# Moving four modulation chunks of layer two from layer one's experts to layer two's attention

## The chip, the cores and the metric

The kernel runs on one core of one Trainium2 chip. The metric is the device time of one execution in microseconds (us), taken as the median of a few runs. "PE" is the tensor engine (matrix products), "PEld" its loading of weights, "DVE" the vector engine, "ACT" the scalar engine, "SP" the engine whose queue issues nearly all loads from memory. The tensor engine's clock has two levels, 1.2 and 2.4 GHz; the profile gives the granted clock as a share of the higher one.

## The reference

Two blocks of two layers each are computed, one behind the other, on 256 tokens of width 1024 in 32-bit floats. The change is in the first block. For each of its layers:

```python
c_act = silu(c)                                  # one row of 1024
mod = c_act @ w_ada[l] + b_ada[l]                # 6 * 1024 numbers
sh_m, sc_m, g_m, sh_f, sc_f, g_f = split(mod, 6)
h = x * (1 + sc_m) + sh_m
mix = token_mixers(h, ...)                       # attention, retention, mLSTM, output product
x = layer_norm(ALPHA * x + (1 + g_m) * mix, ln_mix_g[l], ln_mix_b[l])
h = x * (1 + sc_f) + sh_f                        # <- shift and scale of the feed forward part
y = moe_ffn(h, ...)                              # router and 16 experts, all computed
x = layer_norm(ALPHA * x + (1 + g_f) * y, ln_ffn_g[l], ln_ffn_b[l])
```

The modulation depends only on `c`, so each of its pieces can be computed at any time before its use. `w_ada[l]` is 1024 x 6144; the kernel cuts it into twelve chunks of 512 columns. Chunks 0 and 1 give `sh_m`, 2 and 3 `sc_m`, 4 and 5 `g_m`, 6 and 7 `sh_f`, 8 and 9 `sc_f`, 10 and 11 `g_f`.

## The kernel before

**One chunk.** A chunk is a load of 2 MB from `w_ada` into one slot of a ring (`load_ada`), then eight DVE instructions that multiply the eight row blocks by `cact` and add them up in `tmp` (`ada`: one `tensor_scalar` and seven `scalar_tensor_tensor`, L1376), then a sum over the 128 partitions on PE: four products of a 128 x 128 piece with a column of ones, each in two passes, so eight entries in the profile (`mix_sum`, L705, in the attention; `expert_sum`, L747, in the experts), then one short DVE instruction that adds the bias column (`sum_columns`). When the last of the four chunks is in, `fold("ffn", ...)` multiplies scale and shift with the gain and bias of the layer norm ahead (three short DVE instructions). Two buffers in `tmp` take turns, so a chunk's accumulation waits for the sum of the chunk two before it.

**Where chunks are done.** Three tuples say it. `EARLY` lists chunks done before anything else (layer one's 0 to 3), `MIXING` the chunks done in a layer's attention, `DURING` the chunks done in the expert loop: expert number, then `("ada", c)` for a chunk of this layer or `("next", c)` for one of the next layer. Before, layer one does 4 to 9 in its attention, and in its experts its own 10 and 11 and layer two's 0 to 3 and 6 to 9; layer two does 4 and 5 in its attention and 10 and 11 in its experts.

**The ring.** All weights but those of the down products pass through the four slots of `gring`, in one fixed order (`ring_order`). Entry n goes into slot n % 4, and its load waits until entry n - 4 has been used (`free_slot`, `last_use`): a projection's weights are free when its product for the second token half is done on PE, a chunk when its accumulation is done on DVE. The SP queue issues loads strictly in this order, so a load that waits holds up all behind it.

**The attention stage.** PE runs a written-out sequence (`pe_first`): projections `idx`, `aq`, `ak`, `av`, `mqk`; then eight attention steps s = 0 to 7. In each, PE computes scores (L860), transposes the probabilities (L868), does the work of `between(s)`, and multiplies by the values (L883). `between` holds halves of the projections `mvo` (s = 0 to 3) and `rqk` (s = 4 to 7, L534), at s = 5 the gate columns (L918), and at s = 7 the first mLSTM scores (`ml_scores(0)`, L928), which need the convolution's result after its SiLU on ACT. Then come `rvg` (L534), the mLSTM and retention heads and the output product (L1006). In layer one `mix_sum(6, 7)` stands at s = 2, `mix_sum(7, 6)` at s = 5, `mix_sum(8, 4)` and `mix_sum(9, 1)` behind; the second number is the PSUM bank. Bank 6 also holds the gate columns before and the second half of `rqk` after `mix_sum(7, 6)`.

DVE runs its own written-out order (`dve_first`): after `att_in(2)` come the two gate sums and `ada_of(6)`; after `att_in(3)` `gate_sums`; after `att_in(4)` `ada_of(7)` and `columns_of(6)`; then `att_in(5)`, `att_in(6)`, `att_out(0)`, `conv(0)`, `conv(1)`, `att_in(7)`, `gate_columns`, `conv(2)`, `columns_of(7)`, the rotation of `rqk`, `conv(3)`; at s = 7 `ada_of(8)`; after the mLSTM weights `columns_of(8)` and `ada_of(9)`. `ada_of(c)` and `columns_of(c)` do nothing when chunk c is not in the layer's tuple. Two things differ in layer two: `gain_and_bias` runs there twice (two passes over 128 x 1024 numbers each, L1373), once behind `gate_sums` and once between `att_in(4)` and `ada_of(7)`, and the small `wr_parts` instruction of layer one, behind `conv(3)`, does not run.

**The expert stage.** For each of 16 experts PE does 48 products for gate and up, 24 for down, and transposes (L651). Where `DURING` has a chunk, `expert_sum` follows the transposes of the next expert.

Of the kernel before, what the change touches and what calls it, by code (L numbers as in the profile page):

```python
# [17 lines left out]
KT = D // P  # L18
# [55 lines left out]

EARLY = ((0, 1, 2, 3), ())
EARLY_K = 1
MIXING = ((4, 5, 6, 7, 8, 9), (4, 5))

IN_DOWN = ("avcv", "ak", "buv", "cqk", "wo0")
DIFF = [(t, h) for t in range(TT) for h in range(DH)]  # L80
# [4 lines left out]
MIX_ORDER = (2, 3, 0, 1)  # L85

DURING = (
    {1: ("ada", 10), 2: ("ada", 11), 4: ("next", 0), 5: ("next", 1), 6: ("next", 2), 7: ("next", 3), 9: ("next", 6),
     10: ("next", 7), 12: ("next", 8), 13: ("next", 9)},
    {1: ("ada", 10), 2: ("ada", 11)},  # L90
)

# [7 lines left out]
def ring_order():  # L100

    order = []
    for l, s in enumerate(FIRST):
        names = {0: "ada0 ada1 ada2 ada3 idx aq ada4 ak ada5 av ada6 mqk ada7 mvo ada8 rqk ada9 rvg wo0 wo1",
                 1: "idx aq ak ada4 av ada5 mqk mvo rqk rvg wo0 wo1"}[l].split()
        for e in range(NE):
            names.append(f"gu{e}")
            if e - 1 in DURING[l]:
                names.append(during(l, e - 1))
        order += [(s, n) for n in names]  # L110
    for s in SECOND:
        order += [(s, n) for n in ["avcv", "aq", "ak", "buv", "cqk", "wo0", "wo1"]]
        order += [(s, f"gu{e}") for e in range(NF)] + [(s, "pg0"), (s, "pg1")]
    return order
# [17 lines left out]
B_ADA, LN_MIX_G, LN_MIX_B, LN_FFN_G, LN_FFN_B = 0, 96, 112, 128, 144  # L132
# [104 lines left out]
def program(nc, ins, out, known):  # L237
    ctx = ExitStack()
    with ctx:
# [166 lines left out]
        av, rvg = buf(TT, N), buf(TT, N)  # L406
# [53 lines left out]
        mod = [sc(KT) for _ in range(4)]  # L460
# [230 lines left out]
        def pe_first(l):  # L691
# [255 lines left out]
            def between(s):  # L947

                if s < 4:
                    half_in_proj("mvo", s // 2, s % 2)  # L950
                if s == 2:
                    if l == 0:
                        mix_sum(6, 7)
                if s == 4:
                    half_in_proj("rqk", 0, 0)
                if s == 5:
                    gate_columns()
                    half_in_proj("rqk", 0, 1)
                    if l == 0:
                        mix_sum(7, 6)  # L960
                if s == 6:
                    half_in_proj("rqk", 1, 0)
                if s == 7:
                    ml_scores(0)
                    half_in_proj("rqk", 1, 1)
# [11 lines left out]
                att_values(s)  # L977
            for h in range(NR):
                half_in_proj("rvg", h // 2, h % 2)
                if h == 2 and l == 0:  # L980
                    mix_sum(8, 4)
                if h == 0:
                    ml_scores(1)
                if h < 2:
                    transposed_rope("rqk", h, 4, 4)
                if h == NR - 1:
                    pe.wait_ge(vector_done, V.at(T, ("read", ("att", "O", 1))))
                    transposed_mix(range(2), A)
                ml_values(h)
                if h + 2 < NR:  # L990
                    ml_scores(h + 2)
# [19 lines left out]
            ret_scores(0)  # L1011
            ret_scores(1)
            output_part(0, 0, "att")
            if l == 0:
                mix_sum(9, 1)
            ret_values(0)
            ret_values(1)
            ret_scores(2)
# [630 lines left out]
        def dve_first(l):  # L1649
# [262 lines left out]
            tt(hflat, hflat, mo, ALU.mult).then_inc(vector_done, V.step())  # L1912
            dve.wait_ge(vector_done, V.now())
            columns_of(9)
            if l == 0:
                fold("ffn", LN_MIX_G, LN_MIX_B, mod[3], mod[2])
            ret_weights(2)
            ret_weights(3)
            head_variance("ml", hn, sq, hs, hv)
# [82 lines left out]
            def read_sum(e):  # L2002
# [3 lines left out]
                kind, c = DURING[l][e - 1]  # L2006
# [3 lines left out]
                else:  # L2010
                    sum_columns(l + (kind == "next"), c, psum[:, 2, 0:4], name)
                    if c == 3:
                        fold("mix", LN_FFN_G + KT * l, LN_FFN_B + KT * l, mod[1], mod[0])
                    if c == 9:
                        fold("ffn", LN_MIX_G + KT * (l + 1), LN_MIX_B + KT * (l + 1), mod[3], mod[2])

            def chunk(e):

# [1143 lines left out]
```

## Time and profile before

| what | us |
| --- | --- |
| runs: lowest, median, highest | 1688.45, 1688.72, 1691.14 |
| profiled execution, first to last instruction (span) | 1680.9 |
| median minus that span | 7.8 |
| PE busy in the span | 1626.5 |
| DVE busy | 1083.0 |
| ACT busy | 715.9 |

The profiled execution has no timed figure of its own beside its span; the 7.8 us is what lies outside the first and last instruction when it is compared with the median of the runs. Times in rows are us from the span's start. A timeline row has start, length, engine, line, operation, output <- input, shapes and count; what stands in square brackets is the engine's idle time just ahead and what ended it.

### The profile page before, as it was taken

To read this page: it belongs to the slowest core of one execution; us is meant where nothing else is said; L and a number is where in the kernel's file an instruction comes from. 1 tells how busy PE (TensorE), PEld (TensorE's weight loads), DVE (VectorE), ACT (ScalarE), POOL (GpSimd) and SP (SyncE) were. 2 spreads that over 40 slices of the span, in tenths; PEclk is the share of its full clock that TensorE was granted. 3 is DMA by queue.
4 is the path that set the end of the run, shared out by engine and by line. 5 is a ranking of instruction groups with operands and counts; after the bars stand their busy time and mean duration, and the time that the engine had idled before them with its cause. 6 is when DMAs were issued, how large, how long until landed. Compare 5 with 4: busy or idle time off the path is not lost.

```text
span 1680.9 us, 19186 instructions
## 1 busy us (share of the span) xinstructions
PE 1626.5 (97%) x7467; PEld 1237.3 (74%) x7467; DVE 1083.0 (64%) x1692; ACT 715.9 (43%) x1105; POOL 0.2 (0%) x4
## 2 busy tenths in 40 slices
PE   6999999999999999999999989899999998999998
PEld 5465577888885655688888878778887887788886
DVE  8676787867656764884545567864546767754446
ACT  1133343434321233433434346754336756643445
POOL 0000000000000000000000000000000000000000
PEclk9999999999999999999999999999999998999999
DMA  9846357878664722556555662146466451444641
GB/s 352 303 180 246 126 189 261 289 262 286 228 231 163 249 107 95 188 200 216 184 175 200 208 176 101 51 152 219 155 212 213 146 190 51 150 151 161 215 165 49
DMA packets 218682, 314.98 MB, mean 187 GB/s; under 512 B 22484, under 2 KB 147804, under 8 KB 218464
## 3 DMA queue, kind: packets, MB, share of 16 engines
q1 hardware_dynamic: 217904, 313.63, 54.3%
q8 instruction: 59, 0.97, 0.2%
q14 instruction: 31, 0.25, 0.0%
q10 hardware_dynamic: 688, 0.13, 0.0%
HBM read 312.70 MB, written 1.05 MB: 187 GB/s over the span
## 4 chain that ended last, share of the span: by engine, by line
PE 84%; DVE 10%; ACT 3%; DMA 1%; issue 1%; SPq 0%; DVEq 0%; ACTq 0%
PE psum L598 18%; PE psum L599 17%; PE psum L600 17%; PE psum L534 9%; PE psum L1006 3%; PE psum L605 2%; DVE gring_parts L1373 1%; PE psum L651 1%; DVE arena L1373 1%; PE psum L1206 1%; PE psum L574 1%; DVE arena L1376 1%; PE psum L517 1%; PE psum L575 1%; PE psum L554 1%
## 5 line engine op out<-in xcount | busy, mean ns | idle before, releaser
L600 PE MATMUL psum<-arena_parts,hT_parts 128*128 128x512 f32 x896 | 352.6, 393 | 0.0
L1373 DVE TENSOR_TENSOR gring_parts<-gring,arena_parts 128x2048 fp32r<-128x2048 f32 (+1 forms) x125 | 278.9, 2271 | 50.7 <-ACT arena_parts L2412 50.3
L2412 ACT ACTIVATE arena_parts<-gring 128x2048 fp32r<-128x2048 f32 (+1 forms) x125 | 231.3, 1904 | 7.0 <-DMA gring<-in_w_up 6.6
L1373 DVE TENSOR_TENSOR arena_parts<-psum,ex_parts 128x256 fp32r<-128x256 f32 x106 | 44.6, 420 | 281.0 <-ACT ex_parts L2412 280.9
L2412 ACT ACTIVATE ex_parts<-psum 128x256 fp32r<-128x256 f32 x106 | 40.5, 382 | 394.2 <-PE psum L651 394.2
L598 PE MATMUL psum<-arena_parts,o_cat_parts 128*128 128x512 f32 x512 | 203.2, 397 | 0.0
L599 PE MATMUL psum<-gring_parts,o_cat_parts 128*128 128x512 f32 x512 | 201.8, 394 | 0.0
L600 PEld LDWEIGHTS psum<-arena_parts,hT_parts 128*128 128x128 f32 x896 | 168.2, 188 | 39.4
L598 PE MATMUL psum<-arena_parts,ex_parts 128*128 128x512 f32 x424 | 177.3, 418 | 0.3 <-DVE arena_parts L1373 0.3
L534 PE MATMUL psum<-gring,hT 128*128 128x512 f32 x384 | 174.7, 605 | 1.8 <-DMA gring<-in_w_in 1.8
L600 PE MATMUL psum<-arena_parts 128*128 128x512 f32 x432 | 169.9, 393 | 0.0
L599 PE MATMUL psum<-dring_parts,ex_parts 128*128 128x512 f32 x424 | 166.6, 393 | 0.0
L599 PE MATMUL psum<-gring_parts,arena_parts 128*128 128x512 f32 x416 | 163.9, 394 | 0.0
L598 PE MATMUL psum<-arena_parts 128*128 128x512 f32 x392 | 155.1, 396 | 0.6 <-DVE gring_parts L1373 0.6
L534 PEld LDWEIGHTS psum<-gring,hT 128*128 128x128 f32 x384 | 71.8, 193 | 82.4 <-issue 79.3
L1376 DVE SCALAR_TENSOR_TENSOR tmp<-gring,cact,tmp 128x512 f32<-128x512 f32 x164 | 123.3, 752 | 7.3 <-DMA gring<-in_w_ada 1.2
L1373 DVE TENSOR_TENSOR dring_parts<-dring,arena_parts 128x2048 fp32r<-128x2048 f32 x54 | 123.5, 2287 | 4.4 <-ACT arena_parts L2412 4.4
L2412 ACT ACTIVATE arena<-psum 128x512 f32<-128x512 f32 (+2 forms) x92 | 50.6, 553 | 158.5 <-PE psum L534 74.5
L598 PEld LDWEIGHTS psum<-arena_parts,o_cat_parts 128*128 128x128 f32 x512 | 96.1, 188 | 22.9 <-DVE hT_parts L1373 0.5
L599 PEld LDWEIGHTS psum<-gring_parts,o_cat_parts 128*128 128x128 f32 x512 | 96.2, 188 | 22.5 <-issue 0.5
L2412 ACT ACTIVATE arena_parts<-dring 128x2048 fp32r<-128x2048 f32 x54 | 103.2, 1912 | 0.0
L600 PEld LDWEIGHTS psum<-arena_parts 128*128 128x128 f32 x432 | 81.1, 188 | 19.2
(268 smaller groups left out, 2371.3 us busy)
## 6 DMA issues: line engine op xcount, KB each, us to landing
gring<-in_w_ffn_in SPq DMA_DIRECT2D x44, 1024.0 KB, 8.8
gring<-in_w_ada SPq DMA_DIRECT2D x20, 2048.0 KB, 9.9
gring<-in_w_in SPq DMA_DIRECT2D x16, 2048.0 KB, 12.7
gring<-in_w_gate SPq DMA_DIRECT2D x32, 1024.0 KB, 7.4
gring<-in_w_up SPq DMA_DIRECT2D x32, 1024.0 KB, 9.8
dring<-in_w_down SPq DMA_DIRECT2D x32, 1024.0 KB, 5.1
dring<-in_w_ffn_out SPq DMA_DIRECT2D x22, 1024.0 KB, 5.0
gring<-in_w_out SPq DMA_DIRECT2D x8, 2048.0 KB, 8.3
```

What stands on the lines that cost most here:

```text
L517: last = nc.tensor.matmul(ps[:, 0:n], hT[:, k, t * P:(t + 1) * P], w[:, k, 0:n], start=k == 0, stop=k == KT - 1)
L534: last = nc.tensor.matmul(ps[:, 0:n], hT[:, k, t * P:(t + 1) * P], w[:, k, 0:n], start=k == 0, stop=k == KT - 1)
L554: nc.tensor.matmul(o, w[:, k % 4, c0:c0 + P], hi[:, :, k, :], start=first and k == 0, stop=False)
L574: nc.tensor.matmul(ps, hi[:, t, k, :], w, start=started and k == 0, stop=False)
L598: nc.tensor.matmul(ps, hi, w, start=start, stop=False)
L599: nc.tensor.matmul(ps, hi, w_rest, start=False, stop=False)
L600: return nc.tensor.matmul(ps, lo, w, start=False, stop=stop)
L605: last = nc.tensor.matmul(ps[0:m, at:at + SEQ], w[:, k, c0:c0 + m], hT[:, k, :], start=k == 0, stop=k == KT - 1)
L1006: last = nc.tensor.matmul(ps, hT[:, k, t * P:(t + 1) * P], gslot(stage, f"wo{h}")[:, k, 0:N], start=k == 0, stop=k == 5)
L1373: return nc.vector.tensor_tensor(o, a, b, op)
L1376: return nc.vector.scalar_tensor_tensor(o, a, s, b, op0, op1)
L2412: return nc.scalar.activation(o, a, ACT.Copy)
```

## The change

Chunks 6 to 9 of layer two leave layer one's `DURING` and join layer two's `MIXING`; the ring order, the sums on PE, and the fold on DVE follow.

```diff
-MIXING = ((4, 5, 6, 7, 8, 9), (4, 5))
+MIXING = ((4, 5, 6, 7, 8, 9), (4, 5, 6, 7, 8, 9))
 DURING = (
-    {1: ("ada", 10), 2: ("ada", 11), 4: ("next", 0), 5: ("next", 1), 6: ("next", 2), 7: ("next", 3), 9: ("next", 6),
-     10: ("next", 7), 12: ("next", 8), 13: ("next", 9)},
+    {1: ("ada", 10), 2: ("ada", 11), 4: ("next", 0), 5: ("next", 1), 6: ("next", 2), 7: ("next", 3)},
     {1: ("ada", 10), 2: ("ada", 11)},
 )
...
-                 1: "idx aq ak ada4 av ada5 mqk mvo rqk rvg wo0 wo1"}[l].split()
+                 1: "idx aq ada4 ak ada5 av ada6 mqk ada7 mvo ada8 rqk ada9 rvg wo0 wo1"}[l].split()
...
                 if s == 2:
-                    if l == 0:
-                        mix_sum(6, 7)
+                    mix_sum(6, 7)
...
-                    if l == 0:
-                        mix_sum(7, 6)
+                    mix_sum(7, 6)
...
-                if h == 2 and l == 0:
+                if h == 2:
                     mix_sum(8, 4)
...
-            if l == 0:
-                mix_sum(9, 1)
+            mix_sum(9, 1)
...
             columns_of(9)
-            if l == 0:
-                fold("ffn", LN_MIX_G, LN_MIX_B, mod[3], mod[2])
+            fold("ffn", LN_MIX_G + KT * l, LN_MIX_B + KT * l, mod[3], mod[2])
...
-                    if c == 9:
-                        fold("ffn", LN_MIX_G + KT * (l + 1), LN_MIX_B + KT * (l + 1), mod[3], mod[2])
```

With it, layer two has the ring order up to its experts that layer one has from `idx` on.

## Rows read from the trace of the kernel before

**Rows 1.** The page, busy us (share) and instructions of each engine.

```profile
PE 1626.5 (97%) x7467; PEld 1237.3 (74%) x7467; DVE 1083.0 (64%) x1692; ACT 715.9 (43%) x1105; POOL 0.2 (0%) x4
```

**Rows 2.** The page, chain that ended last, shares by engine.

```profile
PE 84%; DVE 10%; ACT 3%; DMA 1%; issue 1%; SPq 0%; DVEq 0%; ACTq 0%
```

**Rows 3.** Windows: stretch, length, busy of PE, PEld, DVE, ACT, POOL, clock, DMA.

```profile
104.39:186.47 82.08, 79.38 (x337) 46.51 (x335) 57.39 (x108) 26.57 (x56) 0.00 (x0) 0.98 0.53 190
581.18:657.68 76.50, 75.64 (x305) 42.87 (x303) 37.83 (x72) 29.26 (x57) 0.00 (x0) 0.98 0.37 127
232.00:500.00 268.00, 267.27 (x1215) 216.46 (x1214) 191.74 (x224) 98.22 (x105) 0.00 (x0) 1.00 0.72 252
```

**Rows 4.** Timeline of PE in layer one's experts, with and without a chunk.

```profile
326.42 0.38 PE L651 MATMUL psum<-cshared,ex 128*128 128x128 f32 x2
326.63 0.95 PE L747 MATMUL psum<-ones,tmp 128*128 128x1 f32 x8
344.48 0.38 PE L651 MATMUL psum<-cshared,ex 128*128 128x128 f32 x2
...
398.66 0.38 PE L651 MATMUL psum<-cshared,ex 128*128 128x128 f32 x2
415.82 0.38 PE L651 MATMUL psum<-cshared,ex 128*128 128x128 f32 x2
```

**Rows 5.** Timeline of PE in layer one's attention.

```profile
129.05 5.31 PE L534 MATMUL psum<-gring,hT 128*128 128x512 f32 x8 [1.78 <-DMA gring<-in_w_in]
...
140.86 0.95 PE L705 MATMUL psum<-ones,tmp 128*128 128x1 f32 x8
...
147.31 0.61 PE L868 MATMUL psum<-cshared,arena 128*128 128x128 f32 x4
148.69 0.69 PE L928 MATMUL psum<-ex,crows 4*128 4x256 f32 x2 [0.77 <-ACT arena L2409]
...
196.07 3.70 PE L1006 MATMUL psum<-gring,hT 128*128 128x512 f32 x8 [0.69 <-ACT hT L2412]
```

**Rows 6.** Timeline of PE in layer two's attention.

```profile
603.01 3.60 PE L534 MATMUL psum<-gring,hT 128*128 128x512 f32 x8
...
619.99 0.69 PE L928 MATMUL psum<-ex,crows 4*128 4x256 f32 x2 [0.71 <-ACT arena L2409]
...
633.97 5.40 PE L534 MATMUL psum<-gring,hT 128*128 128x512 f32 x8
...
667.28 3.70 PE L1006 MATMUL psum<-gring,hT 128*128 128x512 f32 x8 [0.69 <-ACT hT L2412]
```

**Rows 7.** Timeline of SP's queue, layer one: the loads of chunk 8 and `rqk`.

```profile
115.93 0.37 SPq L2933 DMA_DIRECT2D gring<-in_w_ada  x1
116.40 0.52 SPq L2933 DMA_DIRECT2D gring<-in_w_in  x1
```

**Rows 8.** Timeline of SP's queue, layer two: the loads of `rqk` and `rvg`.

```profile
565.74 0.99 SPq L2933 DMA_DIRECT2D gring<-in_w_in  x2
```

**Rows 9.** Timeline of DVE in layer one: chunk 6, `att_in(7)`, `columns_of(7)`, end of `conv(3)`.

```profile
110.36 5.47 DVE L1376 SCALAR_TENSOR_TENSOR tmp<-gring,cact,tmp 128x512 f32<-128x512 f32 x7
...
136.56 0.69 DVE L1376 SCALAR_TENSOR_TENSOR arena<-psum,arena 128x512 f32<-128x512 f32 x1 [1.49 <-PE psum L868]
...
141.92 0.16 DVE L1373 TENSOR_TENSOR small<-psum,pcol 128x4 f32<-128x4 f32 x1 [1.73 <-PE psum L705]
...
144.68 1.53 DVE L1376 SCALAR_TENSOR_TENSOR arena<-arena,pcol 128x256 f32<-128x256 f32 x3
```

**Rows 10.** Timeline of DVE in layer two: one of two `gain_and_bias`.

```profile
592.28 2.48 DVE L1373 TENSOR_TENSOR x<-x,rows 128x1024 f32<-128x1024 f32 x2
```

**Rows 11.** Windows (columns as in group 3): the granted clock behind layer one's wait.

```profile
129.00:132.00 3.00, 2.95 (x4) 1.40 (x5) 2.83 (x6) 2.87 (x10) 0.00 (x0) 0.50 1.01 378
```

**Rows 12.** Timeline of PE in the second block: a transposition behind a wait.

```profile
1067.42 0.96 PE L1182 MATMUL psum<-cshared,arena 128*128 128x128 f32 x4 [1.34 <-ACT arena L2412]
```

## The prediction

> **What bounds the kernel now.** I read the page first. PE is busy for 1626.5 of 1680.9 us [rows 1] and carries 84% of the chain that ended last, DVE 10% [rows 2]. So each us of PE work or PE waiting on that chain counts in full, and DVE work counts only where PE ends up waiting for it. Then I read the two stages that the change touches by windows. In layer one's experts PE is busy for 267.27 of 268.00 us, with DVE at 191.74 [rows 3]: there is almost no wait to win. In the attentions the two windows run from the transpositions and sums ahead of the eight steps to the third attention part of the output product, the same work in both layers but for what this change moves. Layer one takes 82.08 us with PE idle for 2.70, layer two 76.50 with PE idle for 0.86 [rows 3]. Layer one already carries chunks 6 to 9 in the very places and ring order that the change gives layer two, so its trace is the best measure of what is added. Last, I read the timelines of PE, DVE and SP side by side, shifted by 581.18 - 104.39 = 476.79 us.
>
> **Removed from the experts.** PE's transpositions mark the experts. With a chunk the distance is 344.48 - 326.42 = 18.06 us, without 415.82 - 398.66 = 17.16 us [rows 4]. The 0.90 us are the sum's own eight products (0.95 long, overlapping their neighbours). Four chunks leave: 4 x 0.90 = 3.60 us gained. DVE loses 4 x (0.5 + 5.5) = 24 us there (one multiply and seven additions, 5.47 for the seven [rows 9]), worth nothing by itself, since PE hardly waits in that stage. The four loads of 2 MB leave too; PE waits for no load there. At the end of the stage the first four loads of layer two now wait only for gate and up products of experts 12 to 15, the last (`ak`) for expert 15's, and PE takes idx, aq and the boundary's norm before it needs `ak`: nothing. Later ring entries fall into the same slots as before, since four entries left and four came in.
>
> **Added to layer two's attention, as layer one shows it.** 82.08 - 76.50 = 5.58 us [rows 3]. It can be split. (a) Four sums at 0.9 = 3.6. (b) PE waits 1.78 for the weights of `rqk` in layer one [rows 5], and not in layer two [rows 6]. The reason is SP's order: chunk 8's load waits for chunk 6's accumulation, and `rqk`, behind it, goes out at 116.40 [rows 7], lands 12.65 us later and is used at once. Layer two has no chunk 8 ahead of it, and issued it at 565.74 [rows 8], 37 us before its use. With the change it would go out at 116.40 + 476.79 - 3.60 and be as late as in layer one; all that precedes (ring, PE, DVE up to chunk 6) is layer one's order with layer one's durations. (c) After its wait layer one's eight products took 5.31 us where 3.60 is usual [rows 5, 6], and the granted clock was 0.50, the lower level of 1.2 GHz [rows 11]: 1.71. (d) Layer two has a slow stretch too, 5.40 for 3.70 at 633.97 with no wait ahead [rows 6]: -1.70. Sum 3.6 + 1.78 + 1.71 - 1.70 = 5.39; the last 0.2 is spread over starts and handovers. The later part costs nothing more: chunk 9 delays the load of the first expert's weights, and ACT's rounding of them, but from the end of the windows to the wait at 196.07 and 667.28 both layers take the same 9.6 us with the same idle of 0.69 [rows 5, 6]. If ACT came later there, PE would wait for the head norm's root, but layer one shows it just in time. The three instructions of `fold` are moved from one place to another on DVE, ahead of a wait for retention scores: nothing.
>
> **What layer one does not show.** DVE in layer two has two `gain_and_bias`, of 2.48 (2.52 with the gap) each [rows 10]: 5.04 us. Before, they stand in the place that chunks 6 and 7 have in layer one. With the change DVE has both. I follow DVE from chunk 6 to the end of `conv(3)`. Layer one: 110.36 to 146.21 = 35.85 us, of which it waits 1.49 and 1.73 [rows 9]; 32.63 of work. Layer two: 32.63 + 5.04 = 37.67, from 110.36 + 476.79 = 587.15, so the end is at 624.82, if DVE never waits; on the way each score that it needs is there 0.5 us or more ahead. PE's first mLSTM scores came 148.69 - 146.21 = 2.48 behind that end in layer one (a table load and SiLU on ACT [rows 5, 9]), so they start at 627.30, against 148.69 + 476.79 = 625.48 by layer one's pattern: 1.82 us later. Behind the waiting scores stand PE's second half of `rqk` and everything after it. So PE's wait there grows from 0.77 to 2.6 us in all; 0.9 of it comes earlier, at the sum of chunk 7: that sum takes bank 6, which DVE's copy of the gate columns frees only behind the late `att_in(7)`: 136.56 - 1.49 + 476.79 + 5.04 = 616.9 for its start, 1.6 for it and the copy, so 618.5, where PE is ready at 140.86 + 476.79 = 617.65. That part is not added a second time, as PE is caught by the same DVE end either way. From there DVE's chunk 8 ends at 630.9, and PE's `rqk` that it needs next at 632.4: DVE is no longer late. The bounds of this term: 0, if some DVE work fits into gaps that I took as gone; 5.04, if all of `gain_and_bias` came through. I take 1.82, the sum of the rows.
>
> **The clock.** Whether it falls is the uncertain part. It fell behind the wait of 1.78 [rows 5, 11], and behind one of 1.34 with thin work around it (a transposition group of 0.96 [rows 12]); it did not fall behind layer one's 0.77, and did fall at 633.97 with none. Layer two now gets waits of 0.9 and about 1.6 within 9 us, with small products between, ahead of the stretch where it fell before. I take one fall behind the `rqk` wait, as in (c), and one in the later stretch, where before there was one too. So the -1.70 of (d) does not apply, and the stage costs 5.58 + 1.82 + 1.70 = 9.10 us. The bounds: no fall at all leaves 9.10 - 3.4 = 5.7; three falls make it 10.8.
>
> The Trainium skill (TensorE: Matmul & The Clock Gate, section "What's actually happening") says that the point at which the clock changes is run-variable, since the gate does not start with the kernel. The trace agrees that equal work can differ: 633.97 fell and layer one's equal products did not.
>
> **Sum.** -3.60 + 9.10 = +5.5 us on the profiled execution's 1680.9, with the 7.8 us outside it unchanged: the median goes from 1688.72 to 1694.2. DVE's and ACT's totals stay what they were. The measurement tells about 0.2%, 3.4 us, from no change.
>
> **Rivals.**
> 1. No second fall of the clock: +5.5 - 1.7 = +3.8, 1692.5. For it: layer one fell only once. Against: the waits at 618 to 627 are longer than layer one's.
> 2. The pair of loads lands later than in layer one. The two issues at 115.93 and 116.40 moved 4 MB in 12.6 us; a load that takes 10% longer in that place adds 1.2: 1695.4. The same with a third fall of the clock is 1697.1.
> 3. The waits don't open up: `rqk` lands in time (it would have to be 1.8 us, 14%, faster than in layer one), so neither the wait nor its fall of the clock comes: 5.5 - 1.78 - 1.71 = +2.0, 1690.7, no change that can be measured. Against it is that every event before is layer one's.
> 4. Faster than before: the four sums hide in waits that PE has in layer two's attention anyway (0.71 and 0.69 [rows 6]), the loads are in time, and the clock no longer falls at 633.97. Then the attention pays 3.6 - 1.4 - 1.7 = 0.5 against 3.60 gained: -3.1, 1685.6. It decides from `rqk` landing before PE asks, and from DVE reaching `conv(3)` by 618. Against it: both waits end on DVE and ACT chains that the chunks lengthen.
>
> The Trainium skill (DMA: Bandwidth & Descriptors, section "Specifications") gives about 358 GB/s as what one core gets from memory. By it the 4.19 MB of the pair would take an estimated 11.7 us of moving alone, and with the start from issue to first byte the wait would be about a us longer than layer one's, as in rival 2. The trace does not support it as a limit: the window at that place averages 378 GB/s [rows 11].
>
> **How the numbers follow.** Forecast 0.46, rival 1 0.25, rival 2 0.08, rival 3 0.16, rival 4 0.05. To each I give 0.7 us of scatter, as the three runs of before lie from 0.3 below to 2.4 above their median. Range: from rival 3's 1690.7 less that scatter, 1690.0, to rival 2's upper value, 1697.0; it leaves out rival 4 and the ends. The forecast's own range is 1693.3 to 1695.1. Slower by over 3.4 us (above 1692.1): the forecast, rival 2 and four fifths of rival 1, 0.74; within: 0.22; faster 0.04.
>
> **What would show it.** In layer one's experts every distance from expert 9 on is 17.16. PE waits some 1.8 us for a load ahead of its first `rqk` product near 602 (all times 3.6 earlier than above), with the clock at 0.5 behind it. DVE has no wait from chunk 6 to `conv(3)`; chunk 7's sum waits about 0.9 and the first mLSTM scores about 1.6. The attention from 577.6 on is 9 us longer than before (7.4 in rival 1). The forecast is wrong if the wait for `rqk` is missing, if `conv(3)` ends before PE has done step 7, or if the expert stage shortens by more than 3.6: then DVE or the loads had cost PE time there that the rows do not show.

## The result and the profile after

| kernel | median us | runs | ratio to before, 95% interval |
| --- | --- | --- | --- |
| before | 1690.23 | 13 | 1 |
| changed | 1697.39 | 13 | 1.0048, 1.0034 to 1.0062 |

The change costs 8.1 us (5.7 to 10.5), where 5.5 were forecast. The time, 1697.39, lies 0.4 us above the range's upper end. The sign was right, the size was not. One execution of the changed kernel, the profiled one, and two of the one before ran disturbed (5684, 4309 and 2026 us): the medians in the table count them, the ratio does not, and it compares 1696.87 with 1688.72. The views below are of a second series of the changed program (1694.11 us, ratio 1.0042, 1.0028 to 1.0055).

The page of the changed kernel: busy time, the granted clock in 40 slices, and the chain that ended last. They answer to [rows 1, 2].

```profile
span 1693.2 us, 19182 instructions
PE 1635.0 (97%) x7467; PEld 1243.8 (73%) x7467; DVE 1083.2 (64%) x1692; ACT 715.8 (42%) x1105; POOL 0.2 (0%) x4
PEclk9999999999999999999999999899999998999999
PE 84%; DVE 10%; ACT 3%; DMA 2%; issue 1%; SPq 0%; DVEq 0%; ACTq 0%
```

PE has the same 7467 instructions and is busy 8.5 us longer. Equal products have become longer; how much of that is the clock is counted below. DVE and ACT are unchanged, as forecast.

The span grew by 1693.2 - 1680.9 = 12.3 us, more than the medians differ. The windows that answer to [rows 3], in the same order. The first and the third are layer one's and layer two's attention, each between the same two instructions as before; the second covers the same times as before:

```profile
104.03:187.98 83.95, 81.12 (x337) 47.19 (x336) 57.39 (x108) 26.56 (x56) 0.00 (x0) 0.96 0.52 186
232.00:500.00 268.00, 267.27 (x1199) 216.00 (x1198) 170.58 (x195) 99.84 (x107) 0.00 (x0) 1.00 0.65 224
580.04:665.67 85.63, 81.38 (x337) 47.06 (x335) 61.89 (x111) 26.27 (x55) 0.00 (x0) 0.96 0.50 182
```

Layer two's attention takes 85.63 - 76.50 = 9.13 us more; 9.10 were forecast. An expert that lost its chunk answers to [rows 4], in PE's timeline:

```profile
417.32 0.38 PE L650 MATMUL psum<-cshared,ex 128*128 128x128 f32 x2
...
434.48 0.38 PE L650 MATMUL psum<-cshared,ex 128*128 128x128 f32 x2
```

An expert has two such rows, so from the first shown to the last is one expert: 434.48 - 417.32 = 17.16 us. From expert 9 on every distance is so, and with a chunk it was 18.06. Four chunks give the forecast 3.60 back.

PE in layer two's attention, which answers to [rows 5, 6]: start of the stage, first half of `rqk`, product with the values of step 4, sum of chunk 7, first mLSTM scores, a projection at the lower clock, and the stage's end.

```profile
580.04 1.88 PE L701 MATMUL psum<-tmp,ones 128*128 128x512 f32 x4
...
605.84 5.40 PE L533 MATMUL psum<-gring,hT 128*128 128x512 f32 x8 [2.93 <-DMA gring<-in_w_in]
611.29 1.10 PE L882 MATMUL psum<-arena 128*128 128x64 f32 x8
...
618.06 0.95 PE L704 MATMUL psum<-ones,tmp 128*128 128x1 f32 x8
...
626.23 0.69 PE L927 MATMUL psum<-ex,crows 4*128 4x256 f32 x2 [1.12 <-ACT arena L2402]
...
640.31 5.26 PE L533 MATMUL psum<-gring,hT 128*128 128x512 f32 x8
...
665.67 3.70 PE L1003 MATMUL psum<-gring,hT 128*128 128x512 f32 x8
```

The `rqk` wait is there, 2.93 rather than 1.78, with the clock fallen behind it (5.40 for 3.60). The mLSTM wait is 1.12, not 1.6 or more, and the sum of chunk 7 doesn't wait. The loads of chunk 8 and `rqk` go out as late as forecast, `rqk` 12.02 us into the stage and 12.01 in layer one (the rows below and [rows 3, 7]). `rqk` is used 13.8 us after its issue, 12.65 in layer one [rows 5, 7]. On SP's queue, against [rows 8]:

```profile
591.58 0.37 SPq L2926 DMA_DIRECT2D gring<-in_w_ada  x1
592.06 0.52 SPq L2926 DMA_DIRECT2D gring<-in_w_in  x1
```

What the forecast did not have is outside this stage. These are windows over stretches where the granted clock (third number from the end) fell, first of the kernel before, then of the changed one. 0.50 is the level of 1.2 GHz, 1.00 that of 2.4; a window that also holds some full clock shows a value between.

```profile
128.00:134.00 6.00, 4.95 (x8) 2.26 (x9) 5.65 (x11) 3.29 (x10) 0.00 (x0) 0.72 1.02 360
634.00:638.00 4.00, 4.00 (x7) 1.70 (x7) 0.44 (x1) 0.00 (x0) 0.00 (x0) 0.57 0.00 0
...
1066.00:1072.00 6.00, 4.47 (x25) 4.27 (x24) 5.54 (x16) 4.07 (x11) 0.00 (x0) 0.72 0.00 0
```

```profile
148.00:152.00 4.00, 4.00 (x8) 1.79 (x7) 2.73 (x4) 1.21 (x3) 0.00 (x0) 0.57 0.00 2
162.00:166.00 4.00, 4.00 (x9) 1.94 (x8) 1.00 (x3) 0.00 (x0) 0.00 (x0) 0.57 0.99 386
506.00:512.00 6.00, 5.00 (x12) 3.33 (x13) 5.34 (x14) 1.08 (x4) 0.00 (x0) 0.72 0.24 90
606.00:610.00 4.00, 4.00 (x6) 1.68 (x7) 3.79 (x7) 0.60 (x2) 0.00 (x0) 0.58 0.27 49
640.00:644.00 4.00, 4.00 (x8) 1.80 (x7) 0.69 (x2) 0.00 (x0) 0.00 (x0) 0.57 1.06 406
...
1076.00:1092.00 16.00, 14.08 (x59) 13.05 (x60) 12.16 (x30) 9.77 (x22) 0.00 (x0) 0.57 0.00 1
```

Layer one's attention, whose code the change leaves alone, falls twice here and once before. The layer boundary falls (506), where before it did not, though PE's waits there are the same in both (1.18 and 1.29 us). In the second block a stretch of 6 us became one of 16, while one of 8 us before (972) is 6 us here (980). Stage by stage the pair of profiles adds up so: up to the end of layer one's attention +1.5 (187.98 against 186.47), experts -3.6, from the boundary to 580.04 +1.0, layer two's attention +9.1, and behind it +4.3 (1027.5 against 1023.2 us); in all +12.3. Windows of 2 us over the whole span count the lost clock, each window's length times one minus its clock: 16.5 us before and 24.8 in the changed kernel. The 8.3 between them are 1.7 each in layer one's attention, at the boundary and in layer two's attention, and 3.1 behind it. They agree with the 8.5 of PE's busy time.

One more number sorts these. For every execution, span x (1 - mean granted clock) is an estimate of the time lost to the lower level, and the rest is about what the program would take without it, waits included. It counts time at the lower level as lost even where PE waits, so it is rough by a us or so. Means over the executions:

| kernel | runs | span less lost | lost to the clock |
| --- | --- | --- | --- |
| before, three series | 23, 26, 23 | 1662.5, 1663.2, 1663.0 | 23.7, 23.8, 22.5 |
| changed, two series | 12, 6 | 1667.2, 1667.7 | 27.5, 24.8 |

Of the 8 us, about 4.5 are work and waits, about 3 more lost clock. The profile of before (16.5 lost) is thus of a lucky execution, 7 us below its program's mean of 23.4, and the changed kernel's (24.8) is 2 below its own of 26.6. So some 5 of the 8.3 us of clock between the two profiles are the choice of executions, and a fall in layer one's attention or in the second block cannot be put down to the change from this pair.

### The profile page after: what moved, and what is told of

Its sections match the earlier page's. It is cut to its first block, busy times and chain, and to the rows that moved or that the text cites. A ratio compares the mean times of both kernels' runs of the same rounds, so it can differ in the third digit from the quotient of the medians.

```text
span 5682.3 us, 19182 instructions
## 1 busy us (share of the span) xinstructions
PE 5662.5 (100%) x7467; PEld 2970.5 (52%) x7467; DVE 1095.4 (19%) x1692; ACT 725.5 (13%) x1105; POOL 0.2 (0%) x4
## 4 chain that ended last, share of the span: by engine, by line
PE 100%; DMA 0%; DVE 0%; ACTq 0%; ACT 0%; issue 0%; SPq 0%; DVEq 0%
PE psum L597 20%; PE psum L599 20%; PE psum L598 20%; PE psum L533 11%; PE psum L1003 4%; PE psum L604 2%; PE psum L1202 2%; PE psum L650 2%; PE psum L574 1%; PE psum L580 1%; PE psum L573 1%; PE psum L516 1%; PE psum L553 1%; PE psum L554 1%; PE psum L555 1%; PE psum L1178 1%
## 5 line engine op out<-in xcount | busy, mean ns | idle before, releaser
L599 PE MATMUL psum<-arena_parts,hT_parts 128*128 128x512 f32 x896 | 979.6, 1093 | 0.0
L533 PE MATMUL psum<-gring,hT 128*128 128x512 f32 x384 | 640.2, 1931 | 0.0
L599 PEld LDWEIGHTS psum<-arena_parts,hT_parts 128*128 128x128 f32 x896 | 383.2, 428 | 349.8 <-issue 349.6
L597 PE MATMUL psum<-arena_parts,o_cat_parts 128*128 128x512 f32 x512 | 564.9, 1103 | 0.0
L598 PE MATMUL psum<-gring_parts,o_cat_parts 128*128 128x512 f32 x512 | 559.7, 1093 | 0.0
L597 PE MATMUL psum<-arena_parts,ex_parts 128*128 128x512 f32 x424 | 494.5, 1166 | 0.0
L599 PE MATMUL psum<-arena_parts 128*128 128x512 f32 x432 | 473.3, 1095 | 0.0
L598 PE MATMUL psum<-dring_parts,ex_parts 128*128 128x512 f32 x424 | 463.8, 1094 | 0.0
L598 PE MATMUL psum<-gring_parts,arena_parts 128*128 128x512 f32 x416 | 454.9, 1093 | 0.0
L597 PE MATMUL psum<-arena_parts 128*128 128x512 f32 x392 | 431.0, 1099 | 0.0
L599 PEld LDWEIGHTS psum<-arena_parts 128*128 128x128 f32 x432 | 185.2, 429 | 168.2 <-issue 168.2
L597 PEld LDWEIGHTS psum<-arena_parts 128*128 128x128 f32 x392 | 168.3, 429 | 153.2 <-issue 151.8
```

The lines of the kernel that those rows point to most:

```text
L533: last = nc.tensor.matmul(ps[:, 0:n], hT[:, k, t * P:(t + 1) * P], w[:, k, 0:n], start=k == 0, stop=k == KT - 1)
L597: nc.tensor.matmul(ps, hi, w, start=start, stop=False)
L598: nc.tensor.matmul(ps, hi, w_rest, start=False, stop=False)
L599: return nc.tensor.matmul(ps, lo, w, start=False, stop=stop)
```

## The experiments

**The two programs again.** No edit. `changed_again`:

> The changed kernel as it is, for a profile that can be laid beside that of before. My theory (the waits): in layer two's attention PE waits about 1.8 us for the weights of rqk at s = 4 with the clock at its lower level behind it, 0.9 us at the sum of chunk 7, 1.6 us ahead of the first mLSTM scores; the stage is 9 us longer and the experts of layer one 3.6 shorter. Rival (the clock alone): the waits are as small as in the kernel before, and the extra time lies in stretches of 1.2 GHz, also outside the attention of layer two. Ratio to before expected 1.003 to 1.006 by both; what the windows show tells them apart.

`before_again`:

> The kernel before, unchanged. Its 13 runs lie in two groups, 1683 to 1684 and 1688 to 1693, and its profile has a span of 1680.9, which belongs to the lower group, as 1.8 us lie outside the span in the runs of the changed kernel. Theory: the groups differ in how often the clock falls, mean granted clock 0.990 in the lower and about 0.986 in the upper. If this profile is of the upper group it has some 6 us more in stretches of the lower level than the first profile. Rival: the groups differ in waits for loads, and the clock is the same. Ratio 1.000 within 0.002 by both.

Measured: changed 1694.11 (1.0042, 1.0028 to 1.0055), before 1688.34 (0.9993, 0.9980 to 1.0007). Of the changed kernel's two theories both hold in part: the waits are there, and so are falls outside layer two's attention. Every run of either has 1.8 us outside its span (1.7 to 1.9 by rounding), so the forecast's 7.8 us does not exist. The profiled execution of before took 1680.9 + 1.8 = 1682.7, among the lowest of that program, whose runs in this series reach from 1682.6 to 1692.9 in step with their mean clock: about 1683 at 0.990, 1688 at 0.986, 1690 to 1693 at 0.984. The second profile of before fell into the lower group again (span 1680.8, clock 0.990, 16.5 lost, in the same stretches), so no profile shows where a slower execution of it falls.

**`rqk` loaded earlier.** Only the ring order of layer two differs from the changed kernel:

```diff
-  1: "idx aq ada4 ak ada5 av ada6 mqk ada7 mvo ada8 rqk ada9 rvg wo0 wo1"
+  1: "idx aq ada4 ak ada5 av ada6 mqk mvo rqk ada7 ada8 rvg ada9 wo0 wo1"
```

> The changed kernel with layer two's ring order changed so that mvo and rqk are loaded ahead of chunks 7 and 8 (aq ada4 ak ada5 av ada6 mqk mvo rqk ada7 ada8 rvg ada9 wo0 wo1): rqk goes out some 27 us earlier. Waits theory: the 1.8 us wait at s = 4 is gone and with it the fall of the clock behind it, so 1.8 to 3.5 us less than the changed kernel, ratio to before 1.002 to 1.003; the wait ahead of the first mLSTM scores grows to some 4.4 us, if PE gets there earlier and DVE does not, which gives 1.8 us back: then only the fall of the clock is won. Rival (the load is hidden by DVE's lateness): no change against the changed kernel.

Measured: 1700.34, ratio 1.0082 (1.0068 to 1.0096), slower than the changed kernel by 6 us, although the wait for `rqk` is gone; neither the theory nor the rival had that. PE (stage start, `rqk`, values of step 4), then the one row of ACT:

```profile
580.99 1.88 PE L701 MATMUL psum<-tmp,ones 128*128 128x512 f32 x4
...
603.71 3.60 PE L533 MATMUL psum<-gring,hT 128*128 128x512 f32 x8
612.25 1.97 PE L882 MATMUL psum<-arena 128*128 128x64 f32 x8 [4.94 <-ACT arena L2405]
```

```profile
610.33 0.51 ACT L2402 ACTIVATE arena<-arena,small 128x256 f32<-128x256 f32 x1 [6.72 <-DVE small L1740]
```

`rqk`'s products start 22.72 us into the stage rather than 25.80, and PE then waits 4.94 for ACT, which waits 6.72 for DVE. Step 4's product with the values starts 31.26 us into the stage, as in the changed kernel, so the 6 us come behind it: the clock falls for longer there.

```profile
610.00:622.00 12.00, 9.75 (x30) 6.61 (x31) 9.72 (x20) 4.80 (x14) 0.00 (x0) 0.57 0.02 9
```

By the split of the executions, `rqk_early` is at 1668.7 without the clock (changed kernel in the same series 1667.7) and loses 30.6 (24.8).

The changed kernel has the same chain, hidden. First DVE there, then ACT:

```profile
599.17 2.48 DVE L1369 TENSOR_TENSOR x<-x,rows 128x1024 f32<-128x1024 f32 x2
...
602.22 5.48 DVE L1372 SCALAR_TENSOR_TENSOR tmp<-gring,cact,tmp 128x512 f32<-128x512 f32 x7
...
608.65 0.69 DVE L1740 TENSOR_REDUCE small<-arena 128x2 f32<-128x512 f32 x1
```

```profile
609.37 0.51 ACT L2402 ACTIVATE arena<-arena,small 128x256 f32<-128x256 f32 x1 [6.72 <-DVE small L1740]
...
610.64 0.60 ACT L2405 ACTIVATE arena<-psum 128x512 f32<-128x512 f32 x1
```

`gain_and_bias` and chunk 7 stand in DVE's order ahead of the maxima of step 5. ACT, in its own order, has the exponentials of step 5 (609.37) ahead of the copy of step 4's transposed probabilities (610.64), and PE's product with the values of step 4 needs that copy. So in `rqk_early` work of step 5 holds up step 4.

**`gain_and_bias` later.** The changed kernel with both passes moved from steps 1 and 2 into the loop over the mLSTM heads, ahead of the fourth head's arguments:

```diff
-                if s in (1, 2) and l:
-                    dve.wait_ge(rows_loaded, rows_count(FIRST[l - 1]))
-                    gain_and_bias(s - 1, ("affine", "in", s - 1))
...
+                if h == NR - 2 and l:
+                    dve.wait_ge(rows_loaded, rows_count(FIRST[l - 1]))
+                    for t in range(TT):
+                        gain_and_bias(t, ("affine", "in", t))
```

> The changed kernel with layer two's two gain_and_bias (5.0 us of DVE) moved from between chunks 6 and 7 to just ahead of the fourth head's mLSTM arguments, where DVE is idle for some 6 us. Waits theory: conv(3) ends 5 us earlier, the waits at chunk 7's sum and ahead of the first mLSTM scores shrink to layer one's 0.8 in all: 1.8 us less than the changed kernel, and up to 3.5 if a fall of the clock goes with them; ratio to before 1.002 to 1.004. Rival (DVE's lateness costs nothing): the same time as the changed kernel, ratio 1.005.

Measured: 1694.3, ratio 1.0037 (1.0023 to 1.0052), as the changed kernel and as the rival said. DVE is no longer late, and `rqk` is:

```profile
580.25 1.88 PE L701 MATMUL psum<-tmp,ones 128*128 128x512 f32 x4
...
606.08 5.40 PE L533 MATMUL psum<-gring,hT 128*128 128x512 f32 x8 [2.95 <-DMA gring<-in_w_in]
611.32 1.00 PE L882 MATMUL psum<-arena 128*128 128x64 f32 x8
```

**Both edits.** `gain_late` with the ring order of `rqk_early`:

```diff
+  1: "idx aq ada4 ak ada5 av ada6 mqk mvo rqk ada7 ada8 rvg ada9 wo0 wo1"
...
+                if h == NR - 2 and l:
```

> Both edits at once on the changed kernel: layer two's mvo and rqk loaded ahead of chunks 7 and 8, and its two gain_and_bias moved to the DVE gap ahead of the fourth head. What the first four runs showed: each edit alone wins nothing, as the load of rqk and the chain DVE att_in(5), ACT exp and probabilities, PE values end within 0.1 us of each other, so taking one away leaves the other (rqk early even 6 us worse: 4.9 us of wait and a long stretch at the lower clock). Theory of two waits that cover each other: with both gone, the attention pays only the four sums and a wait of some 1.4 us ahead of the first mLSTM scores; 2 to 3 us less wait than the changed kernel and one fall of the clock less: ratio to before 1.000 to 1.002. Rival (the price is DVE's 24 us of chunks, wherever they stand): ratio stays at 1.004.

Measured: 1696.4, ratio 1.0046 (1.0031 to 1.0061), the rival's number. Nothing is gained, because a third wait takes the place: with `rqk` early in the ring, chunk 7 is late. DVE waits for it, ACT and PE behind:

```profile
601.46 0.49 DVE L1365 TENSOR_SCALAR tmp<-gring,cact 128x512 f32<-128x512 f32 x1 [4.28 <-DMA gring<-in_w_ada]
```

```profile
580.60 1.88 PE L701 MATMUL psum<-tmp,ones 128*128 128x512 f32 x4
...
611.05 1.97 PE L882 MATMUL psum<-arena 128*128 128x64 f32 x8 [4.13 <-ACT arena L2406]
```

**Neither late.** `gain_late` with `mqk` ahead of chunk 6 and `rqk` ahead of chunk 8, chunk 7 staying ahead of `mvo`, so that chunk 7 and `rqk` are both in time:

```diff
-  1: "idx aq ada4 ak ada5 av ada6 mqk ada7 mvo ada8 rqk ada9 rvg wo0 wo1"
+  1: "idx aq ada4 ak ada5 av mqk ada6 ada7 mvo rqk ada8 ada9 rvg wo0 wo1"
```

> The changed kernel with gain_and_bias late as before, and another ring order for layer two: chunk 6 and mqk change places, chunk 8 and rqk change places (av mqk ada6 ada7 mvo rqk ada8 ada9), so that rqk waits for mqk's use (580) and chunk 7's load still goes out at 564. In the kernel both, rqk was in time, but chunk 7's load had moved behind chunk 6's accumulation and DVE waited 4.3 us for it, which came back as 4.1 us of PE waiting for the probabilities of step 4. Theory (one chain of waits, each covering the next): now no load is late and DVE's work ahead of att_in(5) is 5 us shorter: no wait at step 4, about 1 us ahead of the first mLSTM scores; waits in the attention of layer two 2.5 us less than in the changed kernel. Span times clock (what is left when the falls are taken off) near before's 1663 plus 1, against 1667 of the changed kernel; ratio to before 1.000 to 1.002. Rival (the chunks cost what they cost in that stage, some 4 us, wherever the waits show): ratio 1.004.

Measured: 1689.33, ratio 1.0009 (0.9994 to 1.0023): what the change cost is gone within what can be told. By the split it is at 1665.0 and loses 22.4, where before is at 1663.0 and 22.5. Its PE rows, and from the kernel before the two that answer to the first and second:

```profile
579.82 1.88 PE L701 MATMUL psum<-tmp,ones 128*128 128x512 f32 x4
...
606.02 1.10 PE L882 MATMUL psum<-arena 128*128 128x64 f32 x8
...
662.10 3.70 PE L1003 MATMUL psum<-gring,hT 128*128 128x512 f32 x8
```

```profile
581.18 1.88 PE L702 MATMUL psum<-tmp,ones 128*128 128x512 f32 x4
...
606.45 1.00 PE L883 MATMUL psum<-arena 128*128 128x64 f32 x8
```

The start of step 4's product with the values, counted from the stage's first row, puts all six side by side:

| kernel | start - stage start | = us | what ends last |
| --- | --- | --- | --- |
| before | 606.45 - 581.18 | 25.27 | PE's own order |
| ring2_late | 606.02 - 579.82 | 26.20 | PE's own order, with chunk 6's sum |
| both | 611.05 - 580.60 | 30.45 | chunk 7's load, DVE, ACT |
| gain_late | 611.32 - 580.25 | 31.07 | `rqk`'s load and the fall behind it |
| changed | 611.29 - 580.04 | 31.25 | both: `rqk`'s load with its fall, and DVE with ACT |
| rqk_early | 612.25 - 580.99 | 31.26 | DVE and ACT |

The load's chain ends at 31.07 and DVE's at 31.26, 0.2 us apart. At this point taking away either gives at most 0.2 us; taking away both gives 31.25 - 26.20 = 5.05. The 0.93 between the first two rows is one sum.

The whole stage, from its first row to the third attention part of the output product, with the lost clock in it by windows of 2 us:

| kernel | stage, us | lost to the clock | difference |
| --- | --- | --- | --- |
| before | 76.50 | 1.7 | 74.8 |
| ring2_late | 82.28 | 3.4 | 78.8 |
| gain_late | 88.34 | 6.8 | 81.5 |
| changed | 85.63 | 3.4 | 82.2 |
| both | 87.33 | 5.1 | 82.2 |
| rqk_early | 89.42 | 6.8 | 82.6 |

Without the clock `ring2_late` gains 3.4 us in the stage over the changed kernel. Of the 4.0 that remain over before, 3.6 are the four sums, which the experts give back.

**Chunks 6 to 9 of layer two computed nowhere.** This prices the chunks in the experts, and leaves part of the computation out: layer two's feed forward part runs with layer one's shift and scale. From the kernel before:

```diff
-    {1: ("ada", 10), ..., 7: ("next", 3), 9: ("next", 6),
-     10: ("next", 7), 12: ("next", 8), 13: ("next", 9)},
+    {1: ("ada", 10), ..., 7: ("next", 3)},
```

> The kernel before with chunks 6 to 9 of layer two left out of layer one's experts and computed nowhere (layer two's feed forward part takes layer one's shift and scale; its loads, accumulations, sums and fold are left out). Theory: only the four sums on PE counted there, so 3.6 us less than before, ratio 0.998, and the distances of the experts 17.16 throughout. Rival: the loads or DVE cost PE more in that stage than its waits show: 0.996 or less.

Measured: 1684.24, ratio 0.9984 (0.9967 to 1.0001), so 2.7 us, between 5.6 and nothing. By the split, the part without lost clock is 1660.3 against 1663.2 in the same series: 2.9, near the 3.60 of four sums. The distances from expert 9 on are 17.16 throughout, as in the changed kernel: 8 MB less to load and 24 us less of DVE work show nothing beyond the sums there. The time alone can't tell 3.6 from nothing or from 5.

**The clock kept up.** To see what the falls cost, idle products (results never read) were put where PE waits anyway: at the layer boundary, ahead of `rqk` in layer one, ahead of the first mLSTM scores, and in the second block. In the kernel before these are 27 products, as two passes each (PE x7521 against x7467); the expectation below says 33, a miscount. Three of the places:

```diff
+        def keep_busy(bank_no, n, at=0, width=SEQ):
+            for _ in range(n):
+                nc.tensor.matmul(psum[:, bank_no, at:at + width], ident, ones[:, 0:width], start=True, stop=True)
...
                 if s == 4:
+                    if l == 0:
+                        pe.wait_ge(scalar_done, A.at(T, ("read", ("mvo", 1))))
+                        keep_busy(5, 3)
                     half_in_proj("rqk", 0, 0)
...
             if l == 0:
+                keep_busy(0, 8)
                 transposed_parts("xT", x, 0, 4, stage, ("x", "in", 0))
...
             places = (0, 1, 6, 7)
+            keep_busy(4, 1)
```

The kernel before with them:

> The kernel before with 33 idle products (identity times ones, 0.44 us each for 256 columns, into PSUM banks that nobody reads) put into PE's known waits: the two layer boundaries, layer one's wait for rqk, the waits ahead of the first mLSTM scores, and five waits at the end of the second block's attention, each group shorter than its wait. Theory (the clock follows PE's recent activity, and the scatter of 1683 to 1693 is falls): the stretches at 1.2 GHz at 129, 972, 1067 and 1415 get shorter or go, mean clock from 0.986 to 0.990 or more, 3 to 8 us less than before, ratio 0.995 to 0.998, and less scatter. Rival (the falls have another cause, as at 633.97 with no wait ahead): the same falls and 0 to 3 us more, ratio 1.000 to 1.002.

Measured: 1676.32, ratio 0.9933 (0.9914 to 0.9953), a larger gain than the 0.995 to 0.998 expected. The same program in a later series, `before_busy_b`:

> before_busy again, as the mark that the three others are laid beside on the same chip: ratio to before 0.993 as measured before, within 0.002.

Measured: 1675.49, ratio 0.9923 (0.9904 to 0.9943). It beats both kernels. Its six runs lie within 2.9 us, where before's 23 of that series lie within 10.5; in the first series they lie within 7.0, and before's 26 within 12.7. Windows over two of the stretches that had fallen, and over layer two's attention:

```profile
128.00:134.00 6.00, 5.25 (x20) 2.85 (x19) 5.65 (x11) 3.29 (x10) 0.00 (x0) 1.00 1.01 360
634.00:638.00 4.00, 4.00 (x18) 2.32 (x17) 0.00 (x0) 1.06 (x2) 0.00 (x0) 1.00 0.00 0
```

```profile
580.39:655.18 74.79, 74.38 (x307) 42.55 (x305) 37.81 (x72) 29.26 (x57) 0.00 (x0) 1.00 0.38 129
```

Lost clock drops from 22.5 to 2.2 us, and in the first series from 23.8 to 4.5. The rest grows by 8.6 (1663.0 to 1671.6); the idle products take PE time too, and how much of the 8.6 is theirs was not separated.

The kernel `both` with such products:

```diff
+                    keep_busy(5, 3)
                     half_in_proj("rqk", 0, 0)
```

> The kernel both with the same idle products (no group at layer two's rqk, where no wait is left). Theory: as before_busy, against both: 3 to 8 us less, ratio to before 0.996 to 1.000. Rival: no less than both. If it is below before_busy, the place of the chunks in layer two's attention is then no worse than in the experts; I expect it 1 to 2 us above.

Measured: 1685.61, ratio 0.9975 (0.9962 to 0.9988). That is 9.3 us above `before_busy`, where 1 to 2 were expected, and the clock still falls between 604 and 616, behind a wait of 2.61 for ACT.

The changed kernel with the products of `before_busy`, and six rather than three ahead of layer two's `rqk`:

```diff
                 if s == 4:
+                    pe.wait_ge(scalar_done, A.at(T, ("read", ("mvo", 1))))
+                    keep_busy(5, 6 if l else 3)
                     half_in_proj("rqk", 0, 0)
```

> The changed kernel with the idle products of before_busy, and six more in layer two's wait for rqk. With the falls of the clock taken out on both sides, its distance to before_busy is what the chunks' place costs in sums and waits alone: by my sum 3.6 (attention) - 3.6 (experts) + 3.3 (waits 2.9 and 1.1 against 0.7) = 3 to 4 us, so 1680 where before_busy has 1676.5, ratio to before 0.995 to 0.996. Rival (the change's 8 us are mostly work or waits and not the clock): 1683 or more, 7 us above before_busy.

Measured: 1685.87, ratio 0.9986 (0.9972 to 1.0000), which is 10.4 us above `before_busy_b`. I had expected 3 to 4 there, and by its number the rival's 7 or more held. But the falls are not out on both sides: these executions lose 8.1 us to the clock on average, `before_busy_b` 2.2 (the profiled one still falls between 1074 and 1082). The rest is 1675.9 against 1671.6, so 4.3 us are work and waits, which is near my 3 to 4, and 5.9 are clock. The rival is not shown by this. The stage in the window view, then PE:

```profile
576.41:660.38 83.97, 81.07 (x352) 48.23 (x350) 61.87 (x111) 26.28 (x55) 0.00 (x0) 1.00 0.52 185
```

```profile
576.41 1.88 PE L706 MATMUL psum<-tmp,ones 128*128 128x512 f32 x4
...
599.13 2.75 PE L500 MATMUL psum<-ones,cshared 128*128 128x256 f32 x12
602.33 3.70 PE L538 MATMUL psum<-gring,hT 128*128 128x512 f32 x8 [0.45 <-DMA gring<-in_w_in]
607.66 1.10 PE L891 MATMUL psum<-arena 128*128 128x64 f32 x8 [1.63 <-ACT arena L2428]
...
622.59 0.69 PE L936 MATMUL psum<-ex,crows 4*128 4x256 f32 x2 [0.68 <-ACT arena L2425]
```

At full clock the stage still takes 83.97 - 74.79 = 9.18 us more than in `before_busy_b`. PE is idle 2.90 there against 0.41, so 2.5 are waits; the six idle products that stand in for waiting are 2.75, the four sums 3.6; that leaves 0.3. With the experts' 3.6 taken off, that is 5.6 in this one profile. And step 4's product with the values starts 607.66 - 576.41 = 31.25 into the stage, exactly as in the changed kernel, although there is no fall behind `rqk`: DVE's chain sets that point. What the fall no longer takes, PE waits (1.63).

`ring2_late` with idle products:

```diff
+            if l:
+                keep_busy(0, 2)
             transposed("xT", x, 0, 4, ("xn", "in", 0) if l else None)
```

> ring2_late with the idle products. Theory: 0 to 1.5 us above before_busy, ratio 0.993 to 0.995. Rival: 4 us above it, as changed_busy.

Measured: 1678.03, ratio 0.9937 (0.9915 to 0.9959), 2.5 us above `before_busy_b`, where 0 to 1.5 above `before_busy` were expected (it is 1.7 above that), and 7.8 below `changed_busy`. By the split it is at 1670.8 and loses 5.3. So of the 7.8 about 5 are work and waits and 3 clock: the two reorderings that remove both chains take back the change's waits, and some lost clock with them.

## Why the prediction was wrong in size

- **Experts, -3.60.** Right: 17.16 for an expert without its chunk, as forecast.
- **Attention, +9.10.** 9.13 in the profile, with partly different terms. The sums are right (0.93 for the one seen alone). The wait for `rqk` was forecast at 1.78 and is 2.93; its load took some 1.1 us longer from issue to use, which is rival 2's mechanism and nearly its size (1.2). The forecast's estimated 11.7 us of moving for the pair of loads is less than the 129.05 - 115.93 = 13.1 from the first issue to the use in layer one [rows 5, 7], so it gave no reason for a wait a us longer; that the wait grew by 1.15 is luck for that estimate. The fall behind it and one later fall came as forecast.
- **DVE lateness, 1.82 at the mLSTM scores.** Right where it was worked out. DVE never waits from chunk 6 on, and `conv(3)` ends 623.75 - 580.04 = 43.71 us into the stage (row below), by the forecast 624.82 - 581.18 = 43.64; the scores start 46.19 in, by the forecast 627.30 - 581.18 = 46.12. That is why the total agreed: with this end fixed, what the load took longer came off the wait at the scores, 1.12 rather than 2.6 in all, and none is at chunk 7's sum. What I missed is a second place where DVE's lateness counts. I followed DVE to the scores that it reads and to `conv(3)`, and not to ACT and from ACT back to PE. Step 4's product with the values starts 5.98 us later in the stage than before (31.25 against 25.27), where my terms gave 25.27 + 0.9 + 1.78 + 1.71 = 29.66; 1.15 of the 1.6 between are the longer wait for the load. The load's chain and DVE's end together there, so they are paid once, and that is why neither edit alone helped. In the changed kernel itself this miss cost nothing that can be told.

```profile
622.23 1.52 DVE L1372 SCALAR_TENSOR_TENSOR arena<-arena,pcol 128x256 f32<-128x256 f32 x3
```

- **The time outside the span, 7.8 us.** Wrong. 1.8 lie outside; the other 6 are executions with more falls than the profiled one. I set a single execution of the fastest group against a median, and called the difference fixed. The difference that I forecast doesn't contain the 7.8, but taking them for fixed hid that the lost clock of one program varies from run to run by as much as the effect.
- **The clock.** This is the step that failed. Its paragraph counts falls in layer two's attention only (+1.7 net) and puts the lost clock of all the rest of the program at no change, without a reason. In the executions of the result the changed kernel loses 27.5 us to the clock, the one before 23.4 in the mean of its three series: +4.1. In the second series of the changed kernel it is 24.8, and over all its executions 26.6, so +3.2. Work and waits are 4.5 rather than 3.8, which is within the roughness of the split. In the pair of profiles the forecast's 5.5 is there up to 665.67 (9.13 - 3.60), if layer one's attention (+1.5) and the boundary (+1.0) are left out, and another 6.8 lie in those two and in the second block, where the work is the same. As said above, much of these 6.8 comes from the lucky profile of before.
- **The range.** Its lower end has 0.7 us of scatter taken off. Its upper end has none added, and stands at 1697.0 where rival 2's upper value had been worked out as 1697.1. With the scatter that was given to each case it would have been 1697.8, above the measured 1697.39. So the range was missed narrowly, and partly by this; the size, 8.1 for 5.5, was missed by the clock.

The Trainium skill (TensorE: Matmul & The Clock Gate, section "What's actually happening") calls the point at which the clock changes run-variable, which the forecast quoted for one place only. The page says it of a kernel's start. Here the scatter of the unchanged program, 1682.6 to 1692.9 in step with its clock, shows it for the whole run.

What stays open: whether the extra 3 us of lost clock belong to the change or to the executions taken (the two series of the changed kernel give 27.5 and 24.8; `ring2_late`, without the long waits, is at before's 22.4, which speaks for the change), why the clock falls at 634 with no wait in front [rows 6], and how the 1.1 us of `rqk`'s longer load come about. The last was not tried.

## What to carry to other kernels

Follow a late engine through every in-order queue behind it, DVE to ACT to PE, and not only to the buffers that it reads itself: an instruction of step 5 can hold up step 4. When a removed wait brings nothing, look for a second chain that ends at the same point, and remove both in one kernel before judging either. Before a forecast is set on a profile, compare its time with the runs: if equal runs scatter in step with the mean clock, the profile is a sample of one group, and a forecast of the median needs the others' falls as well.

## What was not expected of the hardware

The kernel before loses some 23 of its 1688 us to the lower clock, behind waits as short as 1.34 us [rows 12] or none at all [rows 6]. The same wait need not bring it down twice: layer one's wait for `rqk`, with the clock at 0.50 behind it in [rows 5, 11], is in the changed kernel a wait of 1.91 with the clock at 1.00 behind it, and the fall comes later, at 148. PE, then the window:

```profile
128.82 3.70 PE L533 MATMUL psum<-gring,hT 128*128 128x512 f32 x8 [1.91 <-DMA gring<-in_w_in]
```

```profile
129.00:132.00 3.00, 3.00 (x8) 1.33 (x9) 2.79 (x7) 2.64 (x8) 0.00 (x0) 1.00 1.04 405
```

27 idle products in known waits of the kernel before leave 2.2 us of it in one series and 4.5 in the other, and are worth 0.77% (0.57 to 0.96) and 0.67% (0.47 to 0.86). The like was worth about 0.5% to the changed kernel (1685.87 against 1694.11), whose waits are longer and end on DVE.
